# Early modulation of a two-block kernel: the slot's pieces as weights, the condition's two columns moving

## The reference, cut to what matters

```python
mod = (c_act @ w_mod + b_mod)[:, None, :]
mod_c = (cc_act @ w_mod + b_mod)[None, None, :]
sh1, sc1, gt1, sh2, sc2, gt2 = jnp.split(mod, 6, axis=-1)
...
h = rmsnorm(x, g_norm1) * (1 + sc1) + sh1
hc = rmsnorm(ctx, g_norm1) * (1 + csc1) + csh1
lat_in, lat_gates = project_heads(h, w_in, ...)
ctx_in, ctx_gates = project_heads(hc, w_in, ...)
```

## Time and profile before

| | |
|---|---|
| time, median of 3 runs | 2644.81 us (2641.72 to 2647.22) |
| time of the profiled execution | 2644.23 us |
| its span, first to last instruction | 2642.4 us |
| PE busy | 2576.4 us (98%), 15294 matmul records |
| PE weight loads busy | 2240.9 us (85%) |
| DVE busy | 1988.1 us (75%) |
| ACT busy | 1321.7 us (50%) |
| DMA | 530.30 MB, mean 201 GB/s |
| mean granted clock of PE | 0.992 |

### The profile page before, as it was taken

One profiled execution on the slowest core, in us unless ns is written; L12 is line 12 of the kernel. 1 busy time (PEld: TensorE's weight loads), 2 busy tenths in 40 slices (PEclk: granted clock), 3 DMA queues, 4 the chain that ended last, 5 costly groups with the idle time before them and its releaser, 6 DMA issues.

```text
span 2642.4 us, 40289 instructions
## 1 busy us (share of the span) xinstructions
PE 2576.4 (98%) x15294; PEld 2240.9 (85%) x15294; DVE 1988.1 (75%) x3108; ACT 1321.7 (50%) x1973; POOL 0.2 (0%) x4
## 2 busy tenths in 40 slices
PE   6899999999999999999999999999999999999999
PEld 2587778888788888888888888888888898988888
DVE  4477888968988888888555777787754898657577
ACT  3334424455555555553445544445444655676564
POOL 0000000000000000000000000000000000000000
PEclk8999999999999999999999999999999999999999
DMA  9876675424555555558555555555555454543543
GB/s 398 314 302 255 255 300 193 144 104 186 202 199 186 186 188 189 190 191 312 186 191 174 203 186 185 188 189 191 195 190 187 166 177 176 192 147 112 196 167 136
DMA packets 114636, 530.30 MB, mean 201 GB/s; under 512 B 8224, under 2 KB 8768, under 8 KB 66000
## 3 DMA queue, kind: packets, MB, share of 16 engines
q1 hardware_dynamic: 110832, 507.54, 53.2%
q10 hardware_dynamic: 3680, 21.05, 2.2%
HBM read 526.46 MB, written 2.10 MB: 200 GB/s over the span
## 4 chain that ended last, share of the span: by engine, by line
PE 72%; DVE 7%; ACT 3%; issue 1%; ACTq 0%; DVEq 0%
PE ps L2294 43%; PE ps L2295 22%; DVE lo L1302 3%; PE ps L2285 1%; PE ps L2287 1%; PE ps L2286 1%; ACT hi L617 1%; PE ps L2730 1%; PE ps L2556 1%; ACT p L1258 0%; DVE R L2015 0%; DVE O L2013 0%; PE ps L2590 0%; PE ps L2593 0%; DVE rs L1307 0%
## 5 line engine op out<-in xcount | busy, mean ns | idle before, releaser
L1302 DVE TENSOR_TENSOR lo<-raw,hi 128x1024 fp32r<-128x1024 f32 x700 | 827.9, 1221 | 388.1 <-ACT hi L617 387.7
L617 ACT ACTIVATE hi<-raw 128x1024 fp32r<-128x1024 f32 x700 | 709.0, 1055 | 635.9 <-PE ps L2295 604.9
L2294 PE MATMUL ps<-x,hi 128*128 128x512 f32 x1376 | 330.6, 392 | 4.3 <-DVE x L1808 4.3
L2294 PEld LDWEIGHTS ps<-x,hi 128*128 128x128 f32 x1376 | 253.6, 189 | 54.0 <-issue 4.5
L2294 PE MATMUL ps<-y,hi 128*128 128x512 f32 x1024 | 250.6, 392 | 0.7 <-DVE y L1722 0.6
L2294 PE MATMUL ps<-xp,hi 128*128 128x512 f32 x1024 | 244.7, 391 | 0.1
L641 ACT ACTIVATE hi<-raw 128x1024 fp32r<-128x1024 f32 x98 | 103.1, 1058 | 249.6 <-DMA raw<-in_weights 107.4
L2294 PEld LDWEIGHTS ps<-xp,hi 128*128 128x128 f32 x1024 | 188.2, 188 | 36.7 <-ACT hi L617 0.3
L2294 PEld LDWEIGHTS ps<-y,hi 128*128 128x128 f32 x1024 | 186.1, 189 | 35.7 <-issue 1.0
L2295 PEld LDWEIGHTS ps<-x,lo 128*128 128x128 f32 x1376 | 176.8, 191 | 7.0
L2295 PE MATMUL ps<-x,lo 128*128 128x256 f32 x1376 | 178.8, 283 | 0.0
(11 more groups left out here) (394 smaller groups left out, 4219.2 us busy)
## 6 DMA issues: line engine op xcount, KB each, us to landing
raw<-in_weights SPq DMA_DIRECT2D x459, 1024.0 KB, 4.8
spare<-in_weights SPq DMA_DIRECT2D x16, 1024.0 KB, 14.4
wlast<-in_weights ACTq DMA_DIRECT2D x16, 1024.0 KB, 5.0
xf<-in_xt SPq DMA_DIRECT2D x4, 1024.0 KB, 9.3
raw<-in_weights SPq DMA_DIRECT2D x4, 768.0 KB, 4.3
R<-in_xt ACTq DMA_DIRECT2D x1, 2048.0 KB, 7.3
out<-R SPq DMA_DIRECT2D x1, 1024.0 KB, 8.8
maskn<-in_maskn ACTq DMA_DIRECT2D x1, 512.0 KB, 3.6
```

The costliest lines, as they stand in the source:

```text
L617: act.activation(HI[p % PAIR][:, c], RAW[p % RING][:, c], ACT.Copy).then_inc(hi_ready, 1)
L1302: dve.tensor_tensor(LO[p % PAIR][:, c], RAW[p % RING][:, c], HI[p % PAIR][:, c].bitcast(F32), ALU.subtract).then_inc(lo_ready, 1)
L2294: return pe.matmul(o, h, pair[:, :, k, :], start=start, stop=False, **kw)
```

## The change

The slot's pieces become the weights. For each row tile m (kt is its place in the condition), each of the four blocks q of 128 outputs, and each group c of 32 outputs, a 128x32 piece of the slot is loaded as weights on the column tile that c names, and the two condition values of that row tile (two columns of `csil`) move. The output is two columns of the bank, on the 32 partitions of c: already the turned form that the bias needs. It accumulates over the row tiles and slots of the round. So `cwin`, `fold`, `mrows`, the copy by ACT and `turn_rows` with its semaphores go, and DVE waits for the slots (`whole_used`) in place of the turn.

```diff
+        def mod_block(t, m, c):
+
+            return front_raw(t, 512 * m + c, 32)
...
             def front_round(r):
 
-                act.wait_ge(sem("whole_used"), 8 * (r + 1))
-                if r:
-                    act.wait_ge(sem("mod_turned"), r)
-                act.activation(mrows[:, :], PS[6 + r % 2][:, :], ACT.Copy).then_inc(sem("mod_rows"), 1)
                 if r:
                     front_split(UNIT[SPLITS[3 * r]])
...
             def modulation(r):
 
-                dve.wait_ge(sem("mod_turned"), r + 1)
-                turned = PS[6 + r % 2][:, 0:32]
+                dve.wait_ge(sem("whole_used"), 8 * (r + 1))
                 own.wait()
                 for g in range(2):
                     j = 16 * g + 4 * r
-                    ins = dve.tensor_tensor(mview[:, j:j + 4, :], turned.rearrange("p (q w) -> p q w", w=8)[:, :, 2 * g:2 * g + 2],
+                    ins = dve.tensor_tensor(mview[:, j:j + 4, :], PS[6 + r % 2][:, 2 * j:2 * j + 8].rearrange("p (q s) -> p q s", s=2),
                                             v("b_mod", j, 4)[:, :, None].to_broadcast([P, 4, 2]), ALU.add)
...
             dve.memset(ones[:, :], 1.0).then_inc(sem("ones_ready"), 1)
-            own.done(dve.memset(cwin[:, :], 0.0))
-            own.wait()
-            dve.wait_ge(sem("c_act"), 1)
-            dve.tensor_copy(cwin[:, :].rearrange("p (k w) -> p k w", w=MW)[:, :, 6:8],
-                            csil[:, :].rearrange("p (k s) -> p k s", s=2)).then_inc(sem("fold_ready"), 1)
             dve.wait_ge(sem("eye_loaded"), 16)
-            dve.tensor_reduce(fold[:, :], eye[:, :].rearrange("p (m c) -> p c m", c=32)[:, 0:8, :], AX, ALU.add).then_inc(sem("fold_ready"), 1)
-            dve.tensor_copy(eyer[:, :], eye[0:64, 0:64]).then_inc(sem("fold_ready"), 1)
+            dve.tensor_copy(eyer[:, :], eye[0:64, 0:64]).then_inc(sem("eyer_ready"), 1)
...
                 for n in range(BLOCKS // 2):
-                    if n == 2 and u in TURNED:
-                        turn_rows(TURNED.index(u))
...
                 for m in range(4):
-                    lo = (4 * (u % 4) + m) * MW + 2 * (3 - g)
-                    ins = pe.matmul(PS[6 + r % 2][32 * m:32 * m + 32, :], cwin[:, lo:lo + 32], front_raw(n, 512 * m, 512),
-                                    start=u == MODS[r][0], stop=u == MODS[r][-1], skip_group_check=True)
+                    kt = 4 * (u % 4) + m
+                    for q in range(4):
+                        j = 16 * g + 4 * r + q
+                        for c in range(0, P, 32):
+                            ins = pe.matmul(PS[6 + r % 2][c:c + 32, 2 * j:2 * j + 2], mod_block(n, m, q * P + c), csil[:, 2 * kt:2 * kt + 2],
+                                            start=u == MODS[r][0] and m + q == 0, stop=u == MODS[r][-1], skip_group_check=True)
                 ins.then_inc(sem("whole_used"), 1)
-
-            def turn_rows(r):
...
-            pe.wait_ge(sem("fold_ready"), 3)
+            pe.wait_ge(sem("c_act"), 1)
+            pe.wait_ge(sem("eyer_ready"), 1)
...
-                if t in TURNED and kind == "mod":
-                    turn_rows(TURNED.index(t))
```

More of the change, by code:

```diff
@@ L54 @@
 FINAL_TURNS = (2, 4, 5, 7, 8, 10, 11, 13)
-MW = 38
 DOWN_SLOTS = (KF + 3) // 4
@@ L345, in build @@
         sel_if = wk("sel_if", P, 148, rows=32)
-        cwin = wk("cwin", KD * MW, 132)
         rowh = wk("rowh", T, 149, F32R, rows=64)
         rowl = wk("rowl", T, 148, F32R, rows=64)
-        mrows = at("mrows", 512, 69.25)
-        fold = wk("fold", 8, 150)
         wsum = [wk("wsum0", 512, 118), wk("wsum1", 512, 120), wk("wsum2", 512, 112), at("wsum3", 512, 69.25),
@@ L2448, in mod_slot @@
                 for m in range(4):
-                    lo = (4 * (u % 4) + m) * MW + 2 * (3 - g)
-                    ins = pe.matmul(PS[6 + r % 2][32 * m:32 * m + 32, :], cwin[:, lo:lo + 32], front_raw(n, 512 * m, 512),
-                                    start=u == MODS[r][0], stop=u == MODS[r][-1], skip_group_check=True)
-                ins.then_inc(sem("whole_used"), 1)
-            def turn_rows(r):
[L2456 to L2461, removed]
+                    kt = 4 * (u % 4) + m
[4 more added lines that the diff above has]
+                                            start=u == MODS[r][0] and m + q == 0, stop=u == MODS[r][-1], skip_group_check=True)
+                ins.then_inc(sem("whole_used"), 1)
             def column_sums(g):
```

## The result

2729.89 us median (2723.38 to 2731.51, 4 runs) against 2643.26 us (2641.49 to 2647.22, 4 runs) on the same chip: ratio 1.0323 [1.0304, 1.0342], 86.6 us slower. The profiled execution is 2729.68 us, its span 2727.9. The forecast was +21, with a range to 2690: the direction and the mechanism were right, the size was not.

A forecast was written before the change was run, and what follows sets the result against it. PE, busy 98% of the span, was taken as the bound. 2.8 + 0.1 - 1.4 - 0.4 + 16.8 - 0.1 + 3.2 = +21.0 us on 2644.23 gave 2665.2, as median 2666; range 2641 to 2690, the forecast's own 2650 to 2686.

The forecast's parts named there:

- the fetch at 2.2 us: In runs of slots, fetching a block of 256 PE instructions takes 2.2 us, so each stall is 1.2 us.
- The transfer of 1.03 us: Moving one 16 KB instruction packet takes 1.03 us under full load; as lower bound of the fetch it gives no stall.
- The upper bound of 3.2 us: Longest instruction fetch allowed for; stalls grow by 14 x 1.0 and round 0 by 6 x 1.0, giving 2686 us.
- Count of stalls: One fewer than slots in each run: 14 before the release, 14 x 1.2 = +16.8 us.
- Round 0: Six slots at 2.2 us each from about 25 us, then DVE follows directly without copy and turn: -0.4 us in all.
- The last run: Its stalls lie in PE's 7.10 us wait for loads; its other four slots there cost at most 0.1 us.
- The release: SP's issue of the loads for the last two slots, at 108.51 us before, was to come at 120 to 130 us.
- Clock, +3.2: Two runs of five slots with stalls in the PE stretch lower the granted clock, 1.6 us each: +3.2 us.
- Pace of the burst: A slot's 128 weight loads at 7.7 ns a pair take 1.00 us against 0.86; 20 slots cost +2.8 us.
- The turn, -1.4: In rounds 1 to 3 the turn no longer cuts a key product's stream, -0.47 us each: -1.4 us.
- The supply does not keep up: Denies the rival that more than one instruction block stands ready, leaving only burst cost: +0.4 us, 2645 us, chance 0.26.
- The slow pace (2710): Rival: PE cannot keep the burst's pace in the slots, 3.6 us each, +65 us, 2710 us; chance 0.07.

The follow-up runs named there:

- the run with more loads: The changed kernel with 64 extra loads of 384 KB issued by GpSimd from the end of round 0 on: 2752.69 us, 1.0407 against the kernel before.
- Round 0 alone: Only round 0 in the new form, rounds 1 to 3 as before the change, with the turn: 2660.73 us, 1.0064 against the kernel before.
- the 64-wide pair of runs: The changed kernel with weight pieces 64 columns wide instead of 32, with 2 columns moving (2696.71 us, 1.0204) and with 32 moving (2671.63 us, 1.0105).
- the last loop run: The changed kernel with 28 of 32 slots looping over their first row tile's matmuls, and 32 columns moving instead of 2: 2669.57 us, 1.0095.
- the loop: The changed kernel with 28 of 32 slots running the first row tile's 16 matmuls four times in a loop: 2680.37 us, 1.0134.
- the order with row tiles between: The changed kernel with row tiles of rounds 1 to 3 placed between the eight products of the key half ahead: 2719.74 us, 1.0286.

## Why the prediction was wrong in size

- **The failed step: the fetch at 2.2 us.** It was taken from the nearest row, a 16 KB load. Measured from block to block are 4.2 us on average at the 14 stalls before the release (3.2 to 6.5, counting 128 records back from each hole), 6.2 us in the first half of round 0 and 5.9 to 7.0 in the last run. The transfer of 1.03 us was right; what I had no row for is the time before it starts and the 1.3 to 1.6 us after it lands. The upper bound of 3.2 us added 1 us because that row's engines were almost free; but 3.2 to 3.5 is what a block takes when no data move, so even the bound was the quiet case, and the front is mostly not quiet, as the run with more loads shows.
- **Count of stalls: right.** 2 + 4 + 2 + 4 + 2 before the release, with 29 more packets where about 32 were forecast. The holes of these runs add up to 36.4 us, 2.6 each, where I had 14 x 1.2 = 16.8.
- **Round 0: sign wrong.** I had 6 slots at 2.2 us and DVE following earlier, -0.4. It starts its first key product at 59.30 in place of 42.08: +17.2, because each block took 6.2 us until about 43 us, with the DMA engines full (share 1.02 from 30.54 to 34.20 us). Round 0 alone gave +16 to 17.
- **The last run: hidden in part only.** The wait of 7.10 us did vanish (0.56 us of it is left at 193.33), but the holes in that run came to 13.7 us. The one of 5.67 us was hidden, as forecast: the load behind it landed only at 193.33. Those of 3.27 and 4.32 us come after the load, with nothing left to hide them:

```profile
191.10 1.67 PE L2440 MATMUL ps<-csil,raw 128*32 128x2 f32 x111 [5.67 <-issue]
193.33 0.43 PE L2440 MATMUL ps<-csil,spare 128*32 128x2 f32 x17 [0.56 <-DMA spare<-in_weights]
197.03 1.88 PE L2440 MATMUL ps<-csil,spare 128*32 128x2 f32 x128 [3.27 <-issue]
203.23 1.67 PE L2440 MATMUL ps<-csil,spare 128*32 128x2 f32 x111 [4.32 <-issue]
```

- **The release moved by more.** The issue for the last two slots, expected at 120 to 130 us, came at 184.00, as all that lies ahead of it was slower:

```profile
184.00 1.39 SPq L587 DMA_DIRECT2D spare<-in_weights  x2
```

- **Clock, +3.2: too small, and only half the cause.** I priced two slow stretches from the earlier trace rows. The key products cost +8.7 net of two turns, so between 9 and 10; of the slots' 16.4 some 6 are the pace (32 x 0.2 us), most of the rest the clock. Around 20 us in all, an estimate. I had laid it to pauses alone; the 64-wide pair of runs shows the clock fall without a pause where two columns move.
- **Pace of the burst: nearly right.** 8.5 ns a pair at the upper clock against 7.7 from the earlier trace rows; what I left out is that it is 13.3 at the lower one.
- **The turn, -1.4: consistent.** With the clock kept up, two key halves with no turn between take 11.1 us (74.90 to 86.01 in the last loop run) against 11.7, 0.6 for one turn where I had 0.47.
- **The rivals.** The supply does not keep up. The slow pace (2710) came nearest in time, by another mechanism: in the loop the same matmuls run without holes. The Trainium skill (Runtime: NRT & Kernel Launch, section Instruction fetch mechanics) calls the fetch hidden and gives PE room for 2048 instructions. The 25 holes contradict the first, and the measurement decides; the room, if it is there, was not filled: the run at 86.12, behind 8 us of key products, stands after 165 records, the rest of its block and one more.

What stays open: why a fetch starts 0.7 to 4.8 us after the block before it began. About 1 us of it is there without data (170.21 above); the run with more loads shows that what comes on top grows with the data, not which queue or engine causes it.

## What to carry to other kernels

Count instructions as well as matmuls: divide those of a dense stretch by 256, and give each block what it took here: 3.5 us in quiet, about 4 as a mean, 6 to 7 where loads fill the engines; where PE uses them up sooner, it stands. Before turning a few wide matmuls into many narrow ones, look at what moves: a stretch of weight loads with two columns behind each ran at the lower clock and took the next products with it. Size a wait that no row shows by the state of the machine in that stretch, not by the nearest transfer in a quiet one.

## What was not expected of the hardware

- A fp32 weight load of 32, 64, 128 columns (on four, two, one column tiles) takes 13.3, 53, 213 ns a record at the lower clock; moving 32 columns in place of 2 behind it cost nothing at 64 wide (29 ns with either at the upper clock).
- A loop on PE costs 0.8 to 1.0 us for four turns, an estimate: slots of 1.9 to 2.1 us less the 1.1 of their records.
- The granted clock of a stretch can mislead: in the order with row tiles between, 60 to 80 us is given as 1.00 while its matmuls follow each other at 0.43 us. That trace has no clock record ahead of 105 us, and a stretch without one reads 1.00: so do 40 to 60 us there, with nearly the work that the changed kernel's 40 to 60 us show at 0.50. The steps between matmuls are the safer reading.

```profile
40.00:60.00 20.00, 7.57 (x429) 6.88 (x428) 4.39 (x11) 4.50 (x9) 0.00 (x0) 1.00 0.68 247
60.00:80.00 20.00, 20.00 (x468) 13.48 (x467) 5.20 (x9) 2.49 (x3) 0.00 (x0) 1.00 0.67 228
```
